# A unit's second weight pair is rounded and split inside the attention's steps (differential, dilated, cross)

## The reference

```python
for i in range(DEPTH):
    h = rms_norm(x, mix_pre_g[i])
    if i % N_MIXERS == 0:
        mix = diff_attention(h, positions, da_w_qkv[j], da_lambda[j], da_subln_g[j], da_w_o[j], lambda_init)
    else:
        mix = dilated_attention(h, positions, db_w_qkv[j], db_w_o[j])
    x = x + rms_norm(mix, mix_post_g[i])
    h = rms_norm(x, xa_pre_g[i])
    x = x + rms_norm(memory_cross_attention(h, mem, mem_g[i], xa_wq[i], xa_wkv[i], xa_wo[i]), xa_post_g[i])
    h = rms_norm(x, ffn_pre_g[i])
    x = x + rms_norm(squared_relu_mlp(h, w_up[i], w_down[i]), ffn_post_g[i])
```

## Time and profile before

| | |
|---|---|
| median of three runs | 1898.31 us (1896.17 to 1899.12) |
| the profiled execution | 1895.64 us |
| its span, first to last instruction | 1893.9 us |
| PE busy | 1856.2 us, 98% |
| PEld busy | 1586.6 us, 84% |
| DVE busy | 1152.4 us, 61% |
| ACT busy | 815.7 us, 43% |
| POOL busy | 378.8 us, 20% |
| mean granted clock of PE | 0.996 |

### The profile page before, as it was taken

One profiled execution on the slowest core, in us unless ns is written; L12 is line 12 of the kernel. 1 busy time (PEld: TensorE's weight loads), 2 busy tenths in 40 slices (PEclk: granted clock), 3 DMA queues, 4 the chain that ended last, 5 costly groups with the idle time before them and its releaser, 6 DMA issues. The chain is left out here.

```text
span 1893.9 us, 28167 instructions
## 1 busy us (share of the span) xinstructions
PE 1856.2 (98%) x10762; PEld 1586.6 (84%) x10762; DVE 1152.4 (61%) x1647; ACT 815.7 (43%) x1433; POOL 378.8 (20%) x303
## 2 busy tenths in 40 slices
PE   9999999999999999999999999999999999999997
PEld 7885578889889898998888788897888898989897
DVE  6967956643787556667642356625474368847474
ACT  5226855434546253552123522225553355435362
POOL 0430005500022314104310033300200000522221
PEclk9999999999999999999999999999999999999999
DMA  4330014402232232422332122320451123233331
GB/s 165 123 100 23 1 45 145 152 16 81 87 101 95 95 111 84 125 71 80 98 115 64 35 89 90 101 66 29 139 178 56 57 78 102 78 112 99 99 107 49
DMA packets 99059, 167.73 MB, mean 89 GB/s; under 512 B 5632, under 2 KB 32384, under 8 KB 98688
## 3 DMA queue, kind: packets, MB, share of 16 engines
q1 hardware_dynamic: 98944, 166.15, 27.7%
HBM read 164.03 MB, written 2.10 MB: 88 GB/s over the span
## 5 line engine op out<-in xcount | busy, mean ns | idle before, releaser
L1246 DVE TENSOR_TENSOR w_lo<-raw,w_hi 128x1024 fp32r<-128x1024 f32 x256 | 332.5, 1322 | 257.2 <-ACT w_hi L738 255.6
L738 ACT ACTIVATE w_hi<-raw 128x1024 fp32r<-128x1024 f32 x256 | 264.7, 1058 | 349.5 <-PE ps L1920 337.8
L1920 PE MATMUL ps<-act_hi,w_lo 128*128 128x512 f32 x860 | 340.6, 396 | 3.3 <-DVE act_lo L1397 1.5
L1920 PE MATMUL ps<-act_lo,w_hi 128*128 128x512 f32 x864 | 336.4, 390 | 0.0
L1920 PE MATMUL ps<-act_hi,w_hi 128*128 128x512 f32 x860 | 335.5, 390 | 0.0
L1920 PEld LDWEIGHTS ps<-act_hi,w_lo 128*128 128x128 f32 x860 | 161.9, 188 | 40.8 <-issue 4.5
L1920 PEld LDWEIGHTS ps<-act_lo,w_hi 128*128 128x128 f32 x864 | 162.7, 188 | 35.0 <-issue 1.9
L1920 PEld LDWEIGHTS ps<-act_hi,w_hi 128*128 128x128 f32 x860 | 161.7, 188 | 34.1
L1920 PE MATMUL ps<-ff_hi,w_lo 128*128 128x512 f32 x448 | 176.6, 394 | 0.0
L1920 PE MATMUL ps<-ff_lo,w_hi 128*128 128x512 f32 x448 | 176.6, 394 | 0.0
L1920 PE MATMUL ps<-ff_hi,w_hi 128*128 128x512 f32 x448 | 176.6, 394 | 0.0
(11 more groups left out here) (252 smaller groups left out, 4029.8 us busy)
## 6 DMA issues: line engine op xcount, KB each, us to landing
raw<-in_db_w_qkv SPq DMA_DIRECT2D x72, 512.0 KB, 3.9
raw<-in_w_up SPq DMA_DIRECT2D x64, 512.0 KB, 3.8
raw<-in_w_down SPq DMA_DIRECT2D x64, 512.0 KB, 3.6
raw<-in_xa_wkv SPq DMA_DIRECT2D x32, 512.0 KB, 3.7
raw<-in_da_w_qkv SPq DMA_DIRECT2D x24, 512.0 KB, 3.9
raw<-in_xa_wq SPq DMA_DIRECT2D x16, 512.0 KB, 3.7
raw<-in_xa_wo SPq DMA_DIRECT2D x16, 512.0 KB, 3.7
raw<-in_da_w_o SPq DMA_DIRECT2D x8, 512.0 KB, 3.6
```

The costliest lines, as they stand in the source:

```text
L738: nc.scalar.activation(w_hi[:, g % 4], raw[:, g % 4], ACT.Copy).then_inc(w_hi_ready, 1)
L1246: nc.vector.tensor_tensor(w_lo[:, g % 4], raw[:, g % 4], w_hi[:, g % 4].bitcast(f32), ALU.subtract).then_inc(w_lo_ready, 1)
L1920: last = nc.tensor.matmul(ps[:, s + m, 0:width], left, right, start=(k == 0 and n == 0 and not early), stop=(k == KT - 1 and n == 2))
```

## The change

At the five units that stand before an attention (the last of `qkv0`, the last of `qkv1a` and of `qkv1b`, and the second of `xq0` and of `xq1`) `second` becomes NEVER, a step that the loop doesn't reach. Pair 1 of the next unit (of `o0`, `qkv1b`, `o1`, `xo0`, `xo1`) is rounded by ACT and split by DVE in an event of the attention's first head. On ACT it stands at the end of step 8 in the differential attention and at the end of step 5 in the others; on DVE it stands one step later, at the end of step 9 and of step 6. PE's, POOL's and SP's programs are the same.

```diff
+NEVER = 9
...
+            def second_pair(u):
+
+                def event(a, h):
+                    if h == 0:
+                        heads_of(4 * u + 1)
+                return event
...
-                       scale=lambda m: rstd_cols[:, m:m + 1], first_steps=(att_d, exp_diff, 2) if n == 1 else None, second=4 if n == 1 else 2,
+                       scale=lambda m: rstd_cols[:, m:m + 1], first_steps=(att_d, exp_diff, 2) if n == 1 else None, second=NEVER if n == 1 else 2,
...
-            attention(att_d, exp_diff, 2, (2, diff_out), (5, diff_root), (7, diff_head))
+            attention(att_d, exp_diff, 2, (2, diff_out), (4, second_pair(UNITS["o0"])), (5, diff_root), (7, diff_head))
...
-                                   second=4 if g == GROUPS - 1 else 2)
+                                   second=NEVER if g == GROUPS - 1 else 2)
...
-                            attention(att_l[h], exp_dilated, 2, (2, dilated_to_y))
+                            attention(att_l[h], exp_dilated, 2, (1, second_pair(UNITS["qkv1b"])), (2, dilated_to_y))
                         else:
-                            attention(att_l[h], exp_dilated, 2, (2, dilated_split),
+                            attention(att_l[h], exp_dilated, 2, (1, second_pair(UNITS["o1"])), (2, dilated_split),
...
-                unit(u + 1, first_steps=(att_x[layer], exp_cross, 2), second=4)
-                attention(att_x[layer], exp_cross, 2, (3, head_split))
+                unit(u + 1, first_steps=(att_x[layer], exp_cross, 2), second=NEVER)
+                attention(att_x[layer], exp_cross, 2, (1, second_pair(UNITS[f"xo{layer}"])), (3, head_split))
...
+            def second_pair(u):
+
+                def event(h):
+                    if h == 0:
+                        rests_of(4 * u + 1)
+                return event
...
-            unit(u + 5, first_steps=lambda: attention(att_d, take_max, probs_diff, range(2)), second=4)
+            unit(u + 5, first_steps=lambda: attention(att_d, take_max, probs_diff, range(2)), second=NEVER)
...
-            attention(att_d, take_max, probs_diff, range(2, att_d.n + 9), (6, diff_scale), (8, diff_rest))
+            attention(att_d, take_max, probs_diff, range(2, att_d.n + 9), (5, second_pair(UNITS["o0"])), (6, diff_scale), (8, diff_rest))
...
-                            attention(a, take_masked, probs_plain, range(2, a.n + 1))
+                            attention(a, take_masked, probs_plain, range(2, a.n + 1), (2, second_pair(UNITS["qkv1b"])))
                         else:
-                            attention(a, take_masked, probs_plain, range(2, a.n + 4), (3, dilated_rest),
+                            attention(a, take_masked, probs_plain, range(2, a.n + 4), (2, second_pair(UNITS["o1"])), (3, dilated_rest),
...
-                attention(a, take_max, probs_plain, range(2, a.n + 5), (4, head_rests))
+                attention(a, take_max, probs_plain, range(2, a.n + 5), (2, second_pair(UNITS[f"xo{layer}"])), (4, head_rests))
```

More of the change, by code:

```diff
@@ L1690, in _ @@
                         for g in range(GROUPS):
-                            unit(u + 2 * GROUPS + g, second=2 if g < GROUPS - 1 else 4, first_steps=None if g < GROUPS - 1 else
+                            unit(u + 2 * GROUPS + g, second=2 if g < GROUPS - 1 else NEVER, first_steps=None if g < GROUPS - 1 else
                                  lambda: attention(a, take_masked, probs_plain, range(2)))
                         if h == 0:
-                            attention(a, take_masked, probs_plain, range(2, a.n + 1))
+                            attention(a, take_masked, probs_plain, range(2, a.n + 1), (2, second_pair(UNITS["qkv1b"])))
                         else:
-                            attention(a, take_masked, probs_plain, range(2, a.n + 4), (3, dilated_rest),
+                            attention(a, take_masked, probs_plain, range(2, a.n + 4), (2, second_pair(UNITS["o1"])), (3, dilated_rest),
                                       *[(k - 1, first_half_rest(k)) for k in range(HALF)])
@@ L1744, in queries @@
                                                        ).then_inc(bank_out[(u + n) % 2], 1)
-                    unit(u + n, queries, between=last_planned if n == 0 else None, second=4 if n else 2, first_steps=None if n == 0 else
+                    unit(u + n, queries, between=last_planned if n == 0 else None, second=NEVER if n else 2, first_steps=None if n == 0 else
                          lambda: attention(a, take_max, probs_plain, range(2)))
```

## The result

| | before | with the change |
|---|---|---|
| median of five runs | 1898.10 us (1896.17 to 1899.12) | 1887.81 us (1886.10 to 1889.22) |
| profiled execution | 1895.64 us | 1889.00 us |
| its span | 1893.9 us | 1887.2 us |
| mean granted clock of PE | 0.996 | 0.995 |

The ratio is 0.9948, with a 95% interval of 0.9938 to 0.9959: 10.3 us less at the median, and 7.8 to 11.8 us less by the interval. The changed file's lines lie 1 to 15 further down: L2082 of before is L2097, L1563 is L1578, L1246 is L1254, L738 is L739.

The account below looks back on a forecast made before the run. PE, busy 98% of the span, was taken to bound the kernel, held at five attention starts. Terms -5.2 - 2 x 1.95 - 2 x 0.9 + 1.2 = -9.7 us gave a median of 1888.6, range 1885.5 to 1892.5 (0.79).

Parts of the forecast that it names:

- What bounds the kernel: Whole kernel: PE is busy 98% of the span, so only its standing or slow running can be gained.
- Start of the differential attention: Steps 1 to 5 of that attention: 5.2 us gained, 2.8 of standing and 2.4 of half clock.
- DVE's order, not its work, holds PE: Differential start: step 1's transposes stand 3.06 us because DVE subtracts pair 1 before the take of step 2.
- Middle of the differential attention: Steps 8 to 10: the take of step 10 comes late, costing 1.2 us, bounds 0.9 and 1.2; ACT's share free.
- Dilated and cross starts: Waits at the two dilated and two cross starts vanish: 1.95 us per dilated (bounds 1.75, 2.0), 0.9 per cross.
- The other middles at no cost: Middles of the dilated and cross attentions: idle holes take the pair, cost 0 for all four, otherwise up to 1.2 each.
- the lag of three steps: Cross middle: DVE's 1.23 us passes its hole of 1.09 by 0.14 us, which this lag was to cover.
- The sum: All places together: -9.7 us, the median going from 1898.31 to 1888.6 us and the profiled execution to 1885.9.
- The signs that the prediction named: Changed profile: step 1 wait under 0.4 us, clock 1.00 from 156 to 166, no new dilated or cross start wait over 0.3.
- The clock argument: Dilated start: transposes after 1.75 us standing took 0.66 us, not 1.12; used against the clock-falls-anyway rival, chance 0.18.

Follow-up runs that it names:

- the run with 12 matmuls: Kernel before with 12 added matmuls in PE's 3.06 us wait at the differential attention's start: 10.85 us to step 5's scores; median 1894.35 us, ratio 0.9988.
- pair 1 ahead of the banks: Kernel before with second=0 for second=4 at the five places on both engines, no event: median 1886.43 us, ratio 0.9947; repeated, 1885.90 us, ratio 0.9943.
- the run with two subtractions: Changed kernel with DVE's subtraction of pair 1 done twice in dilated and cross middles: first dilated 43.27, second 43.77, first cross 35.86 us; single run 1888.67 us.
- the best place of the middle: Changed kernel with pair 1 one step earlier in the differential attention alone: that attention 102.80 us, median 1887.35 us over four runs.

## Why the prediction was right

*What bounds the kernel.* Right. The five stretches and the two chance falls of the clock account for the whole difference of the spans; all the rest together is under 0.1 us.

*Start of the differential attention.* Predicted 5.2 us, 2.8 standing and 2.4 clock; measured at the scores of step 5 5.39, by the run with 12 matmuls 2.8 and 2.6. Both parts were confirmed separately. Of it 107.85 - 102.79 = 5.06 is left at the attention's end where nothing was paid in the middle. One reading was only half of it: "DVE's order, not its work, holds PE". In the earlier trace rows DVE is idle until ACT's rounding is done, 1.7 us past the end of step 2's scores, and with DVE's order as it was and the rounding earlier the whole 5.06 us came back. PE was held by the order of ACT and DVE together; the number didn't depend on it, since the change moves both.

*Middle of the differential attention.* Predicted 1.2, bounds 0.9 and 1.2; measured 103.79 - 102.79 = 1.00. The mechanism was right, `take` of step 10 is the instruction that comes late, though the wait came in two parts, 0.96 and 0.49 us. Two errors of 0.1 to 0.2 us cancel in the net, 4.06 against 4.0, which is luck.

*Dilated and cross starts.* Predicted 1.95 and 0.9, measured 2.12 and 0.81 each. The 2.12 lie a little above the bound of 2.0.

*The other middles at no cost.* Right: with pair 1 ahead of the banks, and so nothing in the middle, the first dilated and cross attentions took 43.27 and 35.22 us, against 43.23 and 35.19 with the change. The prediction used the first dilated hole, 2.53 us, for both; the second was 1.93, which still holds 1.23. The reason given for the cross attention, that the lag of three steps covers the rest, was too generous: the run with two subtractions put it at about 0.7 us, enough for the 0.14 needed.

*The sum.* -9.7 predicted, -9.9 by stretches, -10.3 by the medians; 1888.6 predicted, 1887.81 measured. Agreement to 0.8 us is better than the runs allow: those of the change spread from 1886.10 to 1889.22. The profiled execution was to take 1885.9 and took 1889.00, with the two chance falls of the clock; a second profile of the same kernel took 1887.12. The signs that the prediction named came: 0.30 us of waiting at step 1, the granted clock at 1.00 from 156 to 166, and no new wait of PE over 0.3 us at the dilated and cross starts.

*The clock argument.* One step of the prediction was weaker than it looked. I held that no fall occurs at the dilated starts, from one execution. In three of four profiles with that wait it did fall at the second of them, for 1.5 us (47.02 against 45.55). In eight profiles without the wait it never did. So the change probably also removes a fall that the profile of before didn't contain. That this is part of why the median of before lies 2.5 us above its profiled execution is argued, not shown, since the timed runs have no trace; another part would be a fall around 950 us (below).

## What to carry to other kernels

Preparatory work for the next stage, queued in front of an attention's second step, cost 2.8 us of standing at the start of the differential attention, more than its own 1.2, although DVE was idle before it, because its input came late from another engine. Ask of such an instruction what it waits for as well as where it stands: giving DVE its input earlier, in the same place of DVE's order, took away the whole cost, and moving DVE's instruction alone took away nearly all of it at the start. If it has to stand among busy steps, look for the idle time of the engine in front of its next instruction, not for the engine's busy share: a step too late cost 1.0 us here. Ahead of the last banks the pair cost no more than in the best place of the middle (102.79 and 102.68 against 102.80 us), and that needed no new code. A wait of TensorE can have a second price in the clock behind it: 2.6 us behind the wait of 3.06, nearly as much as the wait; behind one of 1.75 us, 1.5 us in three of four profiles at one place and nothing at another.

## What the runs showed of the hardware

The clock's falls are not the same in each execution of the same program. The changed kernel was profiled twice: around 14 us it fell in one execution and not in the other, whose scores of step 2 start at 151.81 us instead of 153.60. Behind the sixteen one-column matmuls of the first column statistic, around 95 us, it fell in eleven of twelve profiles; behind those of the second it fell in every profile but that of before. In the changed kernel, the timeline and the windows:

```profile
945.48 2.91 PE L2076 MATMUL ps<-ones,rstd 1*128 1x1 f32 x16
```

```profile
948.00:950.00 2.00, 2.00 (x6) 1.62 (x7) 0.00 (x0) 0.18 (x1) 0.00 (x0) 0.63 0.89 289
950.00:952.00 2.00, 2.00 (x6) 1.59 (x5) 0.00 (x0) 0.00 (x0) 0.00 (x0) 0.51 0.38 144
```

PE is busy by the records throughout, in the 2.91 us in front of the fall with single columns only. From the start of these sixteen to the scores of step 2 of the first dilated attention the changed kernel needed 1.6 us more than the one of before (945.48 to 1030.34 against 948.26 to 1031.54). A profile of one execution therefore hides or shows some 1.5 us per such place, and differences between kernels of that size are better read from stretches than from spans.
